# Gathering the rows of each expert unit with matmuls from tokens on chip, in place of a list of rows in device memory

## The reference

```
def grouped_moe(h, router_w, router_b, w_gate, w_up, w_down):
    aff = jax.nn.sigmoid((h @ router_w).astype(jnp.float32))
    biased = aff + router_b.astype(jnp.float32)
    ...            # one of 4 groups, then its top 2 experts; weights normalised
    y = jnp.zeros_like(h)
    for e in range(N_EXPERTS):
        he = jax.nn.silu(h @ w_gate[e]) * (h @ w_up[e])
        y = y + combine[..., e:e + 1] * (he @ w_down[e])
    return y
```

## Time and profile before

| what | us |
|---|---|
| median of 3 timed runs | 970.78 |
| lowest, highest | 969.52, 971.41 |
| span of the profiled execution, first to last instruction | 969.1 |
| PE busy in it | 807.4 (83%) |
| DVE, ACT, POOL busy | 405.9, 178.4, 43.1 |
| mean bytes moved | 330 GB/s, 320 MB in all |

### The profile page before, as it was taken

One profiled execution on the slowest core, in us unless ns is written; L12 is line 12 of the kernel. 1 busy time (PEld: TensorE's weight loads), 2 busy tenths in 40 slices (PEclk: granted clock), 3 DMA queues, 4 the chain that ended last, 5 costly groups with the idle time before them and its releaser, 6 DMA issues.

```text
span 969.1 us, 18246 instructions
## 1 busy us (share of the span) xinstructions
PE 807.4 (83%) x6990; PEld 435.3 (45%) x6991; DVE 405.9 (42%) x944; ACT 178.4 (18%) x383; POOL 43.1 (4%) x71
## 2 busy tenths in 40 slices
PE   8899999997979856996668977799879879697674
PEld 3544646444554423553234543374445535353332
DVE  3267879867879841221011223533522111122315
ACT  3222010325630201111001110330211110111002
POOL 0100000130001010000000001000010000000010
PEclk9799989998999897998778989799899989798878
DMA  9989977999506797859999999994779999999971
GB/s 341 361 305 351 336 266 266 332 347 336 199 1 235 300 404 271 350 223 418 415 418 415 355 406 411 391 416 162 276 293 397 371 414 417 414 417 413 415 302 54
DMA packets 99192, 320.22 MB, mean 330 GB/s; under 512 B 10161, under 2 KB 24417, under 8 KB 82609
## 3 DMA queue, kind: packets, MB, share of 16 engines
q1 hardware_dynamic: 75648, 282.49, 74.3%
q0 software_dynamic: 4864, 22.03, 6.1%
q10 hardware_dynamic: 18624, 14.96, 4.7%
HBM read 303.84 MB, written 24.12 MB: 338 GB/s over the span
## 4 chain that ended last, share of the span: by engine, by line
PE 43%; DMA 25%; DVE 12%; SPq 11%; issue 4%; ACT 3%; ACTq 1%; POOL 1%; DVEq 0%; POOLq 0%
DMA raw<-in_w_up 10%; SPq L479 9%; DMA arena<-unit_rows 9%; PE bank L1824 9%; PE bank L1603 7%; PE bank L1837 4%; PE bank L1593 3%; PE bank L1745 3%; PE bank L1998 3%; PE bank L1607 2%; DMA consts_sb<-in_constants 2%; DMA unit_rows<-arena,row_i 2%; DMA arena<-ada_sums 1%; PE bank L1612 1%; PE bank L1539 1%
## 5 line engine op out<-in xcount | busy, mean ns | idle before, releaser
L1824 PE MATMUL bank<-raw,arena 128*32 128x256 f32 x3392 | 241.8, 428 | 65.2 <-DMA raw<-in_w_up 33.8
L1824 PEld LDWEIGHTS bank<-raw,arena 128*32 128x32 f32 x3392 | 118.0, 121 | 170.0 <-DMA raw<-in_w_up 46.9
L1369 DVE TENSOR_TENSOR arena<-arena,bank 64x256 f32<-64x256 f32 x53 | 22.5, 425 | 340.3 <-ACT arena L815 340.3
L1837 PE MATMUL bank<-raw,arena 128*32 128x256 f32 x1696 | 113.1, 397 | 10.2 <-DVE arena L1357 10.2
L1837 PEld LDWEIGHTS bank<-raw,arena 128*32 128x32 f32 x1696 | 59.6, 115 | 50.1 <-DVE arena L1357 11.1
L1603 PE MATMUL bank<-ring,arena 128*128 128x512 f32 x160 | 69.9, 594 | 0.0
L1811 PE MATMUL bank<-consts_sb,arena 64*128 64x64 f32 x212 | 36.5, 295 | 36.6 <-DVE arena L1369 36.5
L815 ACT ACTIVATE arena<-bank 64x256 f32<-64x256 f32 x53 | 19.9, 376 | 254.5 <-PE bank L1824 217.5
L928 DVE SCALAR_TENSOR_TENSOR bias<-ring,small,bias 128x512 f32<-128x512 f32 x77 | 57.9, 752 | 2.7
L1811 PEld LDWEIGHTS bank<-consts_sb,arena 64*128 64x128 f32 x212 | 29.0, 196 | 48.7 <-DVE arena L1369 41.7
L928 DVE SCALAR_TENSOR_TENSOR arena<-ring,small,arena 128x512 f32<-128x512 f32 x63 | 47.4, 752 | 2.2
(11 more groups left out here) (269 smaller groups left out, 856.4 us busy)
## 6 DMA issues: line engine op xcount, KB each, us to landing
raw<-in_w_gate SPq DMA_DIRECT2D x64, 1024.0 KB, 21.0
raw<-in_w_up SPq DMA_DIRECT2D x64, 1024.0 KB, 23.3
raw<-in_w_down SPq DMA_DIRECT2D x64, 1024.0 KB, 22.3
ring<-in_ada_w SPq DMA_DIRECT2D x24, 2048.0 KB, 13.0
ring<-in_w_in SPq DMA_DIRECT2D x7, 2048.0 KB, 13.2
unit_results<-arena ACTq DMA_DIRECT2D x220, 32.0 KB, 7.2
arena<-unit_rows ACTq DMA_DIRECT2D x55, 128.0 KB, 6.9
ring<-in_w_out SPq DMA_DIRECT2D x2, 2048.0 KB, 42.6
```

The lines of the kernel that those rows point to most:

```text
L1824: ins = mm(ps[4][o:o + S, 0:FW], xT[:, i, j * S:(j + 1) * S], w[:, k % 4, h * FW:(h + 1) * FW], start=(k == 0), stop=(k == KD - 1))
L1837: ins = mm(ps[5][j * S:(j + 1) * S, 0:XW], hT_e[:, k % QN, k // QN * S:(k // QN + 1) * S], w[:, k % 2, j * XW:(j + 1) * XW], start=(k == 0 ...
```

## The change

The table `unit_rows`, its filling, `send_rows` and `load_x` go. The normed tokens `f_` stay on chip until the layer's units are through. For each unit n DVE builds a selection `chosen` (128 tokens x 2 x 32 rows of 0 and 1) from the tokens' slots (`choose`, three small instructions), and PE multiplies it with `f_` in eight column-tiled matmuls of 256 columns (`gather_ahead`, sixteen instructions, as `gather` did for units 0 and 1), two units ahead. ACT copies the gathered rows from PSUM (`x_in_psum` in place of `x_landed`).

PE's order within a unit changes: `turn_x(n+1)` now stands before `down(n-1)`, and the gather behind it; on DVE `turned` stands before `result`. The fetched results land in two halves of the weight buffers, since `f_` is still in use, the row numbers for the fetch are computed later (in `weigh`), and the filling of `unit_results` waits for a point in the mixing (`b_ready`).

```
             def fetch_results(l):
                 pool.wait_ge(rows_chosen, l + 1)
-                for t in range(TT):
-                    for q in range(2):
-                        pool.indirect_dma_start(xg, bass.IndirectOffsetOnAxis(row_i[:, 2 * t + q:2 * t + q + 1], 0),
-                                                f_[:, t, :], None).then_inc(rows_out, 16)
...
-                def load_x(n):
-                    act.dma_start(xs[:, 0:XW],
-                                  xg[bass.ds((n + 1) * S, S), :].rearrange("s (j c) -> (s j) c", j=JN)
-                                  ).then_inc(E["x_landed"], 16)
...
                     nc.scalar.activation(sg[64:P, :], ps[4][0:64, 0:FW], ACT.Silu).then_inc(E["silu_done"], 1)
-                    act.wait_ge(E["xT_in_psum"], n + 2)
-                    act.wait_ge(E["x_landed"], n * 16 + 16)
-                    nc.scalar.copy(xs[:, XW:2 * XW], xs[:, 0:XW]).then_inc(E["x_ready"], 1)
-                    act.wait_ge(E["x_ready"], n + 3)
-                    load_x(n + 3)
+                    act.wait_ge(E["x_in_psum"], n + 3)
+                    nc.scalar.copy(xs, ps[6][:, 0:XW]).then_inc(E["x_ready"], 1)
...
-                act.wait_ge(rows_out, 16 * 2 * TT * (l + 1))
-                load_x(2)
                 act.wait_ge(count_ready, l + 1)
...
+                def choose(n):
+                    dve.wait_ge(E["ahead_steps"], n * 2 - 3)
+                    nc.vector.tensor_tensor(both, cst("iota")[:, 0:S].rearrange("p (a s) -> p a s", a=1).to_broadcast(
+                        [P, TT * 2, S]), ahead_s.rearrange("p t (q a) -> p (t q) a", a=1).to_broadcast(
+                        [P, TT * 2, S]), ALU.is_equal).then_inc(E["ahead_steps"], 1)
+                    dve.wait_ge(E["ahead_steps"], n * 2 - 2)
+                    nc.vector.tensor_scalar(ahead_s, ahead_s, float(S), None, ALU.subtract
+                                            ).then_inc(E["ahead_steps"], 1)
+                    dve.wait_ge(E["x_in_psum"], n)
+                    nc.vector.tensor_tensor(chosen, of_q[:, :, 0, :], of_q[:, :, 1, :], ALU.add
+                                            ).then_inc(E["chosen_ready"], 1)
...
                     product(n)
+                    turned(n + 1)
                     result(n - 1, place, stores)
-                    turned(n + 1)
+                    choose(n + 3)
...
+                def gather_ahead(n, closes):
+                    pe.wait_ge(E["chosen_ready"], n - 1)
+                    gather(6, chosen, closes)
...
                 def turn_he(n):
                     pe.wait_ge(E["he_ready"], n + 1)
+                    pe.wait_ge(E["xT_ready"], n + 2)
...
                     gate_up(n, own, begins)
+                    pe.wait_ge(E["hT_ready"], n)
+                    turn_x(n + 1)
                     down(n - 1, prev)
-                    turn_x(n + 1, begins)
+                    gather_ahead(n + 2, begins)
```

More of the change, by code:

```diff
@@ L265, in program @@
                           ("slot", (TT, 2)), ("share", (TT, 2)), ("rel", (TT, 2)), ("late_share", (TT, 2)),
-                          ("late_at", (1,))], KD * W + 6 * D + NE * UN)
+                          ("late_at", (1,)), ("row", (TT, 2)), ("ahead", (TT, 2)), ("both", (TT * 2, S)),
+                          ("chosen", (TT, S))], KD * W + 6 * D + NE * UN)
         assert at <= MODS
@@ L273, in program @@
             "parts", "comb", "some", "runA", "runB", "slots", "pick", "slot", "share"))
-        rel, late_share, late_at = (me[n] for n in ("rel", "late_share", "late_at"))
+        rel, late_share, late_at, row_f, ahead_s, both, chosen = (me[n] for n in (
+            "rel", "late_share", "late_at", "row", "ahead", "both", "chosen"))
         ys, Pg, Ph = (lay([("ys", (4, XW)), ("Pg", (TT, 2 * S)), ("Ph", (TT, 2 * S))], 2 * D)[0][n]
                       for n in ("ys", "Pg", "Ph"))
-        y_of = ([f_[:, t, :] for t in range(TT)], [bias[:].rearrange("p a n -> p (a n)"), arena[:, 3 * D:4 * D]])
+        fetched0 = [halves[s][:].rearrange("p (t n) -> p t n", t=TT) for s in FETCH_AT]
+        y_of = [([fetched0[l][:, t, :] for t in range(TT)], [bias[:].rearrange("p a n -> p (a n)"),
+                                                            arena[:, 3 * D:4 * D]]) for l in range(2)]
         fT = lay([("fT", (KD, SEQ))], KD * W + 4 * D)[0]["fT"]
@@ L380, in program @@
             L.append({n: sem(f"{n}{l}") for n in (
-                "x_ready", "x_landed", "xT_in_psum", "xT_ready", "gate_up_done", "silu_done",
+                "x_ready", "x_in_psum", "ahead_steps", "chosen_ready", "xT_in_psum", "xT_ready", "gate_up_done", "silu_done",
                 "he_ready", "hT_in_psum", "hT_ready", "y_in_psum", "y_ready", "y_stored0", "y_stored1", "y_stored2", "y_stored3",
                 "expert_begun", "expert_closed")})
+        y_back, added = [sem(f"y_back{t}") for t in range(TT)], sem("added")
         rows_filled = sem("rows_filled")
-        y_back, added = [sem(f"y_back{t}") for t in range(TT)], sem("added")
-        rows_chosen, rows_out, p_ready, x_in_psum = (sem(n) for n in (
-            "rows_chosen", "rows_out", "p_ready", "x_in_psum"))
+        rows_chosen, p_ready = sem("rows_chosen"), sem("p_ready")
         late_diag, late_in_psum, late_ready, scattered, further_stored = (sem(n) for n in (
@@ L576, in fetch_results @@
                     for q in range(2):
-                        pool.indirect_dma_start(y_of[q][t], None, yg,
+                        pool.indirect_dma_start(y_of[l][q][t], None, yg,
                                                 bass.IndirectOffsetOnAxis(row_i[:, 2 * t + q:2 * t + q + 1], 0)
                                                 ).then_inc(y_back[t], 16)
-            fills = ([(xg, r, min(r + SEQ, ROWS)) for r in range(0, ROWS, SEQ)]
-                     + [(yg, r, min(r + SEQ, ROWS)) for r in range((LATE + 1) * S, ROWS, SEQ)])
+            fills = [(r, min(r + SEQ, ROWS)) for r in range((LATE + 1) * S, ROWS, SEQ)]
             pool.wait_ge(bias_zero, 2)
@@ L600, in _ @@
                 if c == FILL_AFTER:
[L601 to L602 removed]
+                    pool.wait_ge(b_ready, 1)
+                    for a, b in fills:
+                        pool.dma_start(yg[a:b, :], x[0:b - a, :]).then_inc(rows_filled, 16)
             load_gain(gmix, 1, 2)
             pool.wait_ge(rows_filled, 16 * len(fills))
[L605 removed]
             for b in range(2):
@@ L1395, in experts @@
                 for n in range(2):
-                    dve.wait_ge(x_in_psum, 2 * l + n + 1)
+                    dve.wait_ge(E["x_in_psum"], n + 1)
                     if n:
                         dve.wait_ge(E["xT_in_psum"], n)
-                    nc.vector.tensor_copy(xs[:, XW:2 * XW], ps[n][:, 0:XW]
-                                          ).then_inc(E["x_ready"], 1)
-                turned(0, False)
+                    nc.vector.tensor_copy(xs, ps[n][:, 0:XW]).then_inc(E["x_ready"], 1)
+                turned(0)
+                nc.vector.tensor_scalar(ahead_s, slot_f, float(2 * S), None, ALU.subtract
+                                        ).then_inc(E["ahead_steps"], 1)
+                choose(2)
                 weigh()
                 product(0)
-                turned(1, False)
+                turned(1)
+                choose(3)
                 further(dve.value_load(cnt_i[0:1, 0:1], min_val=0, max_val=SEQ))
@@ L1878, in experts @@
                 pe.wait_ge(p_ready, l + 1)
-                gather(0)
-                gather(1)
-                turn_x(0, False)
+                for n in range(2):
+                    gather(n, Pg[:, :, n * S:(n + 1) * S], False)
+                turn_x(0)
                 pe.wait_ge(count_ready, l + 1)
@@ L1885, in experts @@
                 gate_up(0, own, True)
-                turn_x(1, False)
+                pe.wait_ge(E["xT_ready"], 1)
+                turn_x(1)
+                gather_ahead(2, False)
                 further(pe.value_load(cnt_i[0:1, 0:1], min_val=0, max_val=SEQ), own, ahead)
@@ L1928, in experts @@
                     gate_up(n, own, True)
-                    turn_x(n + 1, True)
+                    turn_x(n + 1)
+                    gather_ahead(n + 2, True)
                     pe.reg_add(units, units, 1)
@@ L1936, in experts @@
                             down(n - 1, own)
-                            turn_x(n + 1, False)
+                            turn_x(n + 1)
+                            gather_ahead(n + 2, False)
                             scatter(n - 1, False)
```

53 lines of the change are left out of this document (27 added, 26 removed).

## The result

The changed kernel takes 974.51 us (median of 20 runs, 970.93 to 977.89); the kernel before, run beside it, 969.75 us (20 runs, 965.57 to 975.96). The ratio is 1.0039, with a 95% interval of 1.0022 to 1.0056: 0.4% slower, where 956.0 us (943 to 967) had been forecast. The profiled execution took 974.29 us with a span of 972.4 us; that of before has a span of 969.1 us.

What follows compares the result with a forecast made beforehand. Weights (DMA) set the time where the DMA is full, PE where weights wait for it; -8.7 us in layer 0 and -6.1 in layer 1 gave -14.8 from 970.78, so 956.0 us (943 to 967).

Steps and rivals of the forecast that it cites:

- the start of layer 0: Layer 0, units 0 and 1: silu no longer waits for the table, so the second gate_up starts at 360.4, -11.2 us.
- now 7 x 7.2 = 50.4: +0.2: Layer 0, units 1 to 7 (experts 1 and 2): 50.2 us before, 50.4 at 7.2 us a unit, +0.2 us.
- The rival of the hidden start: Layer 0: units 1 and 2 now wait for weights, taking half of the 11 us; 961.5 us, chance 0.11.
- units 1 to 5 of layer 1: Layer 1, up to 751.46: 37.1 us before, now 5 x 7.2 = 36.0, so -1.1 us.
- The other -1.1 of that start: Layer 1: the second gate_up follows the first after 6.9 us, not 8.0, -1.1 us.
- the end of layer 0: Transfer issued when expert 15 begins: PE's 1.95 us wait at 616.02 gives way to PE's own chain, -1.9 us (0 to -1.9).
- the +2.5: Layer 0, expert 11 to expert 15's gate_up: four gathers of 0.93 us added, less covered waits, +2.5 us (0 to 3.7).
- the unit's price: PE, each unit: 6.34 us less about 0.1 plus 0.93 for the gather, 7.17, or 7.27 with another shape change; 7.2 taken.
- The upper price for draining (7.58): PE, turn_x: 0.41 us of idle paid once more per unit, 7.58 us; as rival of dearer units 965.5 us, chance 0.14.
- the row loads: Where DMA is full: 128 KB less per unit, 0.32 us each; -2.5 us in layer 0, -5.8 (18 loads) in layer 1.
- DVE costed at nothing: Each unit: waits of turn_x for `turn_back` and turn_he for `turned` are covered by some 2 us, so cost nothing.
- The rival in which DVE becomes the bound: Each unit: PE waits for DVE; decides from 7.79 us a unit, 981 us with 1 us of wait; chance 0.07.

Runs made afterwards that it cites:

- slot 0: Changed kernel with PE's code from each layer's mixture part on loaded at slot 0 of a 256-instruction block, nothing computed differently: 957.92 us, ratio 0.9875 to the kernel before.
- slot 128: Changed kernel with PE's code from each layer's mixture part on loaded at instruction 128 of a 256-instruction block: 965.54 us, ratio 0.9948 to the kernel before.
- the five slots that were tried: Changed kernel with PE's mixture code loaded at instruction 0, 32, 64, 128 or 192 of a 256-instruction block: 957.92, 962.38, 961.77, 965.54 and 977.69 us.
- slot 192: Changed kernel with PE's code from each layer's mixture part on loaded at instruction 192 of a 256-instruction block: 977.69 us, ratio 1.0066 to the kernel before.

## Why the prediction was wrong

The us by which each point comes earlier (-) or later (+) than in the kernel before, by the prediction's sum, in the changed kernel and at slot 0. At slot 0 the rows of PE for these points are

```profile
363.46 3.66 PE L1837 MATMUL bank<-raw,arena 128*32 128x256 f32 x64
...
417.76 3.66 PE L1837 MATMUL bank<-raw,arena 128*32 128x256 f32 x64
...
515.49 3.66 PE L1837 MATMUL bank<-raw,arena 128*32 128x256 f32 x64
...
551.85 0.42 PE L1837 MATMUL bank<-raw,arena 128*32 128x256 f32 x4
...
599.84 3.66 PE L1837 MATMUL bank<-raw,arena 128*32 128x256 f32 x64
...
611.20 3.83 PE L1973 MATMUL bank<-arena,consts_sb 128*128 128x512 f32 x8
...
697.87 3.66 PE L1837 MATMUL bank<-raw,arena 128*32 128x256 f32 x64 [0.92 <-DVE arena L1338]
704.86 3.66 PE L1837 MATMUL bank<-raw,arena 128*32 128x256 f32 x64
...
744.32 1.06 PE L1837 MATMUL bank<-raw,arena 128*32 128x256 f32 x14
```

| point | prediction | changed | slot 0 |
|---|---|---|---|
| layer 0, second gate_up | -11.2 | -6.1 | -8.2 |
| layer 0, expert 3 begins | -11.0 | +3.7 | -4.1 |
| expert 10, second unit | -12.6 | +0.6 | -6.9 |
| expert 11 begins | -9.3 | +4.2 | -3.3 |
| layer 1, first gate_up | -8.7 | +5.1 | -8.5 |
| layer 1, expert 3 begins | -10.9 | +9.9 | -7.1 |
| end of the span | -14.8 | +3.3 | -13.5 |

- **Wrong: the start of layer 0**, "gate_up(1) starts at 360.4 instead of 371.62: -11.2", and behind it "now 7 x 7.2 = 50.4: +0.2". The step that failed is the path: it counted the data alone and gave PE's own instructions a price of nothing. The data were ready at 359.77, which with turn_he is the 360.4 of the forecast, though by luck: the first gate_up came 1.3 us later (354.69 against 353.44), and the 3.3 us behind it held 1.3 for a table load that ACT had done before (at 352.52 in the changed kernel). At the two jumps of 3.60 and 5.19 us PE stood still for 4.77 and 4.96 us, and the gate_up behind each took 1.8 and 1.6 us more: 13.1 of the 14.7 us that are missing when expert 3 begins. Not all of the first wait is the coming of code. At slot 128, where that jump takes 0.47 us, 1.63 us of wait stay ahead of turn_he, in which the sequencer loads registers; these had no price either. The rival of the hidden start had the place and not the cause: it named weights, and the gate_ups at 365.53 and 379.71 wait for none.
- **Wrong, in the same way: units 1 to 5 of layer 1**, "now 5 x 7.2 = 36.0: -1.1". They took 42.9 us (718.38 to 761.31), with waits of 1.55 and 2.67 us for code and a slow gate_up behind the second. The other -1.1 of that start came out: the second gate_up follows the first after 6.94 us in the changed kernel and after 6.99 at slot 0, where 6.9 had been forecast, again with a wait of PE's sequencer (1.33 us) in the room of the table load.
- **Wrong in sign: the end of layer 0**, -1.9 for the transfer: the wait for the transfer went, but the jump of 6.10 us at expert 15 took its place (623.20 against 616.02, from 606.61 against 600.78: +1.4). From expert 11 to expert 15 the +2.5 came out as +1.6.
- **Right: the unit's price**, 7.27 us (7.2 forecast; 7.27 is what the sum gave with the extra change of shapes), at every address. The upper price for draining (7.58) is not met. The page of the Trainium skill behind it (TensorEngine Tiling (Array Packing), Tiling Modes, Key Properties) says that a change of the tiling mode drains the engine; 7.27 exceeds the sum without such a change by 0.10 us, and no run here takes the drain by itself.
- **Right as far as shown: the row loads**, -5.8 forecast in layer 1, -7.0 measured (+9.9 at expert 3, +2.9 at the last half), and in layer 0 -3.1 from expert 3 to the second unit of expert 10, where -1.6 (-2.5 + 0.9) had been forecast. No run takes the row loads away by themselves.
- **Right: DVE costed at nothing.** The rival in which DVE becomes the bound does not show: no full-clock unit waits for DVE in these rows.

That the kernel at slot 0 comes out at 957.9 us, 1.9 from the forecast, is in part chance. It still loses 7 us against the sum by expert 3, and from expert 11 to layer 1 it gains 5.2 us where the sum had a loss of 0.6. Of that, 3.9 us lie between the gate_up of expert 15 and the transfer (599.84 to 611.20, and 600.78 to 616.02 in the kernel before), where -1.9 had been forecast, and 1.6 ahead of the first gate_up of layer 1, where the wait for the copied rows is 0.92 us in place of 2.27; the sum had nothing there. Some 2 us lie between the two, and 2.3 us go the other way, from expert 11 to expert 15. Here is a stretch of 60 us with the Fourier part in it (busy us by engine, PEclk, DMA share, GB/s), of the kernel before

```profile
640.00:700.00 60.00, 56.95 (x207) 30.04 (x205) 26.34 (x81) 11.88 (x35) 0.00 (x0) 0.94 0.67 264
```

and of the changed one at slot 0

```profile
635.00:695.00 60.00, 54.18 (x213) 28.90 (x216) 27.90 (x89) 11.18 (x34) 0.55 (x1) 1.00 0.71 279
```

The granted clock is 0.94 in the one and 1.00 in the other.

So the change is worth 1.3% at the best of the five slots that were tried, near what was forecast and in part for other reasons, and less than nothing at the address where it happened to be put. What stays open is how the fetch itself chooses: which blocks are kept, when a packet sets out, and why an announced jump still waits.

## What to carry to other kernels

A long wait that goes away uncovers everything that was done under it. Beside data, that is the coming of code: where PE enters code for the first time by a jump over a large body, reckon with a wait until the trace shows none (on the first pass here the jumps took 0.3 to 6.2 us), and look at the sequencer's own rows (jumps, register loads) ahead of the place. And a change that alters the length of PE's code should be timed at two or three addresses before it is judged: here the address is worth 20 us, more than the change at its best address.

## What was not expected of the hardware

- One conditional jump, that of expert 14 in layer 0, took 0.43 us at slot 128 and 6.24 at slot 192, by its address alone; PE's wait behind the longer one was 6.17 us.
- The code of a loop stays: in layer 0 the jumps of the loop of three experts take over 0.3 us only in the first pass, and no packet of q8 is recorded from 437 to 577 us in the changed kernel, nor from 397 to 570 us in the kernel before.
- The announcement of a jump made no difference that shows: 4.46 and 2.46 us without it in layer 0, 4.05 and 2.56 with it.
- Standing still can cost twice: the gate_ups behind the waits of 4.77 and 4.96 us took 5.50 and 5.24 us in place of 3.66. The length of the wait does not settle it: at slot 0 gate_up took 3.66 us behind 2.67, at slot 128 5.35 behind 1.63.
